# Rotary halves stacked, convolution taps in PSUM and on TensorE, and the memory's norm moved in a two-block transformer

## The reference

```python
def mla_mixer(x, ...):                    # 16 heads, 128 + 64 (rotary) columns
    ...
    scores = (jnp.einsum('bqhc,bkc->bhqk', ql, ckv)
              + jnp.einsum('bqhr,bkr->bhqk', qr, k_rope)) * scale
    probs = jax.nn.softmax(scores.astype(jnp.float32), axis=-1)
    return jnp.einsum('bhqk,bkc->bqhc', probs, ckv)

def diff_attention(q, k, v, lam):         # 4 heads, two components of 64 each
    ...
    sc = jnp.einsum("bhcqd,bhckd->bhcqk", q_blk, k) * scale
    sc = jnp.where(mask, sc, -jnp.inf)    # causal
    p = jax.nn.softmax(sc, axis=-1)
    a = p[:, :, 0] - lam * p[:, :, 1]
    return jnp.einsum("bhqk,bhkv->bhqv", a, v)

def hybrid_mixer(h, ...):
    ...
    q = partial_rope(q, positions)        # k likewise
    a = rmsnorm(diff_attention(q, k, v, lam), subln_g) * (1.0 - lam_init)
    c = u[..., :CV_WIDTH] * jax.nn.sigmoid(u[..., CV_WIDTH:])
    c = causal_dwconv(c, cv_dw_w) + cv_dw_b      # 512 channels, 31 taps
    c = jax.nn.silu(layernorm(c, cv_ln_g, cv_ln_b))
    return jnp.concatenate([a, c], axis=-1) @ w_out

def cross_attention(h, m, w_cq, w_ckv, w_co):    # m = rmsnorm(mem, norm_mem_g)
    kv = jnp.einsum("bmd,de->bme", m, w_ckv)
    ...
```

## Time and profile before

| | |
|---|---|
| median of three runs | 2626.41 us (2624.59 to 2631.72) |
| the profiled execution | 2628.91 us, its span 2627.1 us |
| granted clock of TensorE, mean over the span | 0.95 |
| busy, TensorE and VectorE | 2420.0 and 1550.6 us |
| busy, GpSimd and ScalarE | 1421.2 and 683.7 us |

### The profile page before, as it was taken

How to read it: one execution, slowest core, us unless ns; L and a number is a source line. 1 busy time by engine, 2 the same in 40 slices (tenths; PEclk the granted TensorE clock), 3 DMA queues, 4 the chain that set the end, 5 groups by cost and what they waited for, 6 DMA issues and landing times.

```text
span 2627.1 us, 26738 instructions
## 1 busy us (share of the span) xinstructions
PE 2420.0 (92%) x10646; PEld 1921.7 (73%) x10646; DVE 1550.6 (59%) x1870; ACT 683.7 (26%) x1223; POOL 1421.2 (54%) x845
## 2 busy tenths in 40 slices
PE   7999988999988899999899999886688899999997
PEld 5888866888876567777778888764466678778786
DVE  6785739335566455155755337678786645655555
ACT  3332322100023355255211001231123322211112
POOL 5445345666646213413466666555976564666663
PEclk9999999999999799899999999997777999999999
DMA  4222222333322101101233333231111232233332
GB/s 146 69 65 76 62 72 76 93 99 97 97 73 68 34 31 48 55 31 56 73 94 97 97 98 97 72 96 48 41 40 49 65 104 65 88 96 97 90 98 77
DMA packets 57436, 199.02 MB, mean 76 GB/s; under 512 B 6368, under 2 KB 7648, under 8 KB 57312
## 3 DMA queue, kind: packets, MB, share of 16 engines
q1 hardware_dynamic: 56160, 194.69, 24.3%
q10 hardware_dynamic: 1152, 2.62, 0.3%
HBM read 195.19 MB, written 2.10 MB: 75 GB/s over the span
## 4 chain that ended last, share of the span: by engine, by line
PE 79%; DVE 14%; ACT 3%; POOL 1%; issue 1%; DMA 0%; DVEq 0%; ACTq 0%; SPq 0%; POOLq 0%
PE bank L393 24%; PE bank L394 23%; PE bank L395 23%; DVE d_acc L1606 3%; DVE uL L1598 2%; PE bank L741 1%; PE bank L736 1%; POOL wL L2315 1%; PE bank L557 1%; PE bank L751 1%; DVE tmp L1598 1%; DVE sums L1598 1%; DVE mq L1598 1%; DVE tmp L1606 1%; PE bank L538 1%
## 5 line engine op out<-in xcount | busy, mean ns | idle before, releaser
L2313 POOL TENSOR_SCALAR wH<-raw 128x1024 fp32r<-128x1024 f32 (+3 forms) x375 | 403.3, 1075 | 1134.2 <-PE bank L395 1106.2
L2315 POOL TENSOR_TENSOR wL<-raw,wH 128x1024 fp32r<-128x1024 f32 (+3 forms) x375 | 910.8, 2429 | 31.3
L393 PE MATMUL bank<-aH,wH 128*128 128x512 f32 x1520 | 615.9, 405 | 73.7 <-ACT aH L1060 36.9
L394 PE MATMUL bank<-aL,wH 128*128 128x512 f32 x1520 | 602.5, 396 | 0.0
L395 PE MATMUL bank<-aH,wL 128*128 128x512 f32 x1520 | 602.3, 396 | 0.0
L393 PE MATMUL bank<-uH,wH 128*128 128x512 f32 x960 | 381.0, 397 | 32.1 <-DVE uL L1598 26.7
L393 PEld LDWEIGHTS bank<-aH,wH 128*128 128x128 f32 x1520 | 292.9, 193 | 150.1 <-issue 36.3
L394 PE MATMUL bank<-uL,wH 128*128 128x512 f32 x960 | 377.9, 394 | 0.0
L395 PE MATMUL bank<-uH,wL 128*128 128x512 f32 x960 | 377.7, 393 | 0.0
L394 PEld LDWEIGHTS bank<-aL,wH 128*128 128x128 f32 x1520 | 292.6, 193 | 65.0 <-issue 4.7
L395 PEld LDWEIGHTS bank<-aH,wL 128*128 128x128 f32 x1520 | 291.4, 192 | 63.1
(11 more groups left out here) (292 smaller groups left out, 3347.6 us busy)
## 6 DMA issues: line engine op xcount, KB each, us to landing
raw<-in_ws SPq DMA_DIRECT2D x341, 512.0 KB, 3.5
raw<-in_ws SPq DMA_DIRECT2D x16, 384.0 KB, 3.0
raw<-in_ws SPq DMA_DIRECT2D x9, 256.0 KB, 2.6
h<-in_xT SPq DMA_DIRECT2D x4, 512.0 KB, 7.0
out<-c_F SPq DMA_DIRECT2D x8, 256.0 KB, 2.1
raw<-in_ws SPq DMA_DIRECT2D x8, 192.0 KB, 2.6
tmp<-in_pT ACTq DMA_DIRECT2D x4, 256.0 KB, 2.8
d_P<-in_memT ACTq DMA_DIRECT2D x2, 512.0 KB, 4.6
```

The source lines that it names most:

```text
L393: P.e.matmul(o, lH, rH, start=start, stop=False, skip_group_check=skip)
L394: P.e.matmul(o, lH, rL, start=False, stop=False, skip_group_check=skip)
L2313: G.e.tensor_scalar(wH[n % NW][:, c], raw[n % NR][:, c], 1.0, 0.0, MUL, ADD).then_inc(*G.did("wH", n, i))
L2315: G.e.tensor_tensor(wL[n % NW][:, c], raw[n % NR][:, c], wH[n % NW][:, c].bitcast(F32), SUB).then_inc(*G.did("w", n, i))
```

## The change

**Latent attention.** Per head one tile m_qr[i] holds the high part of the rotary columns in one half of the partitions and the low part in the other; m_krH and m_krL hold the keys' columns in both halves. Two matmuls of 128 rows replace the three of 64. Per pair of heads ScalarE and VectorE do one half-height operation more. The division by the sum goes from ScalarE to GpSimd, four instructions per head, put into GpSimd's queue ahead of a chosen weight split.

The scaling ahead of the permutation is gone, and nearly every instruction has one operand in a bank. The core of the diff:

```diff
@@ scores, TensorE
-                    P.e.matmul(b.ap[:, :], m_qrH[r, c], m_krH[r, :], start=False, stop=False)
-                    P.e.matmul(b.ap[:, :], m_qrH[r, c], m_krL[r, :], start=False, stop=False)
-                    P.e.matmul(b.ap[:, :], m_qrL[r, c], m_krH[r, :], start=False, stop=True).then_inc(*P.did("ms", hd, n))
+                    P.e.matmul(b.ap[:, :], m_qr[hd % 2][:, c], m_krH[:, :], start=False, stop=False)
+                    P.e.matmul(b.ap[:, :], m_qr[hd % 2][:, c], m_krL[:, :], start=False, stop=True).then_inc(*P.did("ms", hd, n))
@@ GpSimd
+            def divide(hd):
+                for n in range(4):
+                    x = m_P[hd % 2][:, n, :]
+                    G.wait_ge(V, "minv", hd, n)
+                    G.e.tensor_scalar(x, x, m_st[:, 4 * (hd % 2) + n, 2:3], 0.0, MUL, ADD).then_inc(*G.did("mP", hd, n))
...
             for n in range(len(PLAN)):
+                if n in divided:
+                    divide(divided[n])
                 split_chunk(n, 2 if n == 0 else 1)
-                for _ in range(200 if n == last else after.get(n, 0)):
-                    next(tap, None)
@@ end of the second MLP's layer, TensorE
                 stat_end("ple", i)
                 P.also("end ple", i)
+                if i == 1:
+                    for o in range(4):
+                        memory_keys(o)
@@ taps, VectorE
+                for i in range(3):
+                    y = bk_acc(i)
                     for k in range(31):
+                            V.wait_ge(V, "tap", i, k - 1)
+                            stt(y, x, wk, y, MUL, ADD).then_inc(*V.did("tap", i, k))
@@ taps of tile 3, TensorE
+                for k in range(k0, k1):
+                    P.wait_ge(A, "dg", k)
+                    P.e.matmul(taps["bank"].ap[:, :], d_dg[k % 4][:, :], d_cp[:, BY_PE, 2 + k:514 + k], start=k == 0, stop=k == 30,
+                               skip_group_check=True).then_inc(*P.did("ctap", k))
@@ rotation, VectorE
+                stt(y, y, s, C[:, :], MUL, MUL).then_inc(*V.did("rc", j))
+                V.wait_ge(P, "rts", j)
+                stt(t, bk("rts", j)[:, :], s, Sn[:, :], MUL, MUL).then_inc(*V.did("rts", j))
+                V.wait_ge(V, "rts", j)
+                tt(y, y, t, ADD).then_inc(*V.did("rr", j))
@@ order of a head, TensorE
             for hd in range(3):
                 d_turned(hd)
                 d_scores(hd + 1)
                 if hd < 2:
-                    rotated(2 * hd + 4)
-                    rotated(2 * hd + 5)
+                    rotary_in(2 * hd + 4)
+                    rotary_in(2 * hd + 5)
+                    memory_keys(4 + hd)
+                    rotate(2 * hd + 4)
+                    rotate(2 * hd + 5)
+                conv_taps(8 + 8 * hd, min(16 + 8 * hd, 31))
                 d_values(hd)
```

More of the change, by code:

```diff
@@ L289, in build, with mlp_memory @@
         mlp_r, mlp_q, mlp_E, tab = [], [], [], []
-        for i in range(2):
+        def mlp_memory(i):
             with ExitStack() as st:
@@ L294, in build @@
                 mlp_E.append(sb(f"E_{i}", [128, 8, T], F32, st))
[L295 removed]
+                tab.append([sb(f"tab{j}_{i}", [128, T], F32, st) for j in range(3)] if i == 0 else
+                           [mlp_E[1][:, 5 + j, :] for j in range(3)])
+        mlp_memory(0)
         with ExitStack() as st:
@@ L1309, in rotate @@
                     A.wait_ge(P, "ms", hd - 1, 3)
-                do(m_qrH[:, :], tmp[1][:, :], ACT.Copy).then_inc(*A.did("qrH", hd))
+                for i in range(2):
+                    j = do(m_qr[i][half_rows(i), :], tmp[1][half_rows(i), :], ACT.Copy)
+                j.then_inc(*A.did("qrH", hd))
             def heads_in(hd):
@@ L1955, in rotate @@
                 V.wait_ge(A, "qrH", hd)
-                low(m_qrL[:, :], tmp[1][:, :], m_qrH[:, :]).then_inc(*V.did("qrL", hd))
+                for i in range(2):
+                    j = low(m_qr[i][half_rows(1 - i), :], tmp[1][half_rows(i), :], m_qr[i][half_rows(i), :])
+                j.then_inc(*V.did("qrL", hd))
             def heads_in(hd):
@@ L2058, in some_taps, with memory_keys @@
                     next(tap, None)
+            def memory_keys(o):
+                V.wait_ge(A, "xkH", o)
+                low(x_kL[:, o, :], bk("xk", o)[:, 0:256], x_kH[:, o, :]).then_inc(*V.did("xkL", o))
+            for o in range(4):
+                memory_keys(o)
             V.wait_ge(A, "rstd", "n", 1)
             for i in range(4):
-                t = tmp[(i + 1) % 2][:, :]
+                a, b = bk("ca", i)[:, :], bk("cb", i)[:, :]
                 V.wait_ge(P, "cb", i)
-                if i == 3:
-                    V.wait_ge(A, "memH", 6)
@@ L2206, in dve @@
             residual("z", "wo", ("z",), lambda k: vv("norm_cross_g_2", k))
-            for o in range(8):
-                V.wait_ge(A, "xkH", o)
-                low(x_kL[:, o, :], x_kF[:, o, :], x_kH[:, o, :]).then_inc(*V.did("xkL", o))
             for half in range(2):
```

505 lines of the change are left out of this document (256 added, 249 removed).

## The result

The changed kernel takes 2549.61 us (median of four runs, 2549.08 to 2551.4) where the kernel before took 2625.62 on the same chip (four runs, 2624.59 to 2631.72): a ratio of 0.9707, with a 95% interval of 0.969 to 0.9724. That is 76 us less, where 98 were forecast. The execution whose profile is read here took 2551.4 us, with a span of 2549.6, so 77.5 less than the profiled one of before.

What follows compares the result with a forecast made beforehand. TensorE was taken to bound latent attention, VectorE's taps differential attention and convolution. Terms -40 + 11 - 33 - 36 = -98 took 2628.9 to 2531, less 2.5 for the median: 2528 us; own range 2512 to 2545, wider 2492 to 2570.

Steps and rivals of the forecast that it cites:

- (a): Rival, latent attention scores: switches don't cost what was thought, so the scores save only 19 us; 2549 us, chance 0.10.
- (c): Rival, differential attention loop: five banks instead of eight give the taps' gain back, loop stays at 193; 2549 us, chance 0.15.
- (1): Latent attention scores: five 128-row matmuls per tile instead of six with switches between 128 and 64 rows; 40 us saved.
- (2): Latent attention: the division of the probabilities moves from ScalarE to GpSimd at no cost.
- (e): Rival, latent attention: GpSimd, waiting for a head's sums, delivers the next split 2 us late per head; 2560 us, chance 0.05.
- (4): Gate's sum to norm's sum: four key tiles put ahead take weight slots, so splits come later; +11 us.
- (5): Norm's sum to differential attention's first scores: VectorE's taps in banks at 0.80 us each; 33 us saved.
- (b): Rival, convolution taps: in a bank they are held by GpSimd as before, 1.3 us each; 2562 us, chance 0.13.
- (f): Rival, slower: VectorE instructions writing a bank are far dearer than ones only reading it; 2665 us, chance 0.03.
- (6): First differential attention scores to the projection's first three tiles: more TensorE work but less standing, 172 us; 36 saved.
- (3): Second MLP: the memory's norm moves there beside a full TensorE; costed at 0 to 1 us.
- (7): After the projection: the key split lies beside full TensorE work; 0 to 2 us, taken as 0.

Runs made afterwards that it cites:

- e1: The changed kernel with the latent attention's rotary stacking taken back (six score matmuls per tile, three of 64 rows); 2593.12 us.
- e2: The changed kernel with the division of the probabilities back on ScalarE; 2545.7 us.
- v2: The changed kernel with memory key tiles moved, differential attention's scores over 128 rows and the division back on ScalarE; 2519.19 us.
- v1: The changed kernel with memory key tiles moved and differential attention's scores over 128 rows; 2526.34 us.
- e5: The changed kernel with memory key tiles moved: one instead of four ahead of the mixer's norm, the others later; 2534.95 us.
- e3: The changed kernel with VectorE's convolution taps added up in SBUF instead of in two banks; 2566.21 us.
- e4: The changed kernel with differential attention's scores over 128 rows, each component's keys zero-padded in the other half; 2541.17 us.
- e6: The changed kernel with 30 of TensorE's 31 tap matmuls cut to a quarter of their columns; 2544.37 us.

## Why the prediction was right, and where its size was off

**Right in direction and in its places.** The gain is VectorE's waiting taken out of differential attention and convolution and TensorE's switches taken out of the scores, as said. The time itself, 2549.6, lies outside the forecast's own 2512 to 2545, on the figure of rivals (a) and (c), and within the wider range only because that reaches over them; neither rival's cause is borne out. By the terms:

(1) Scores, -40 forecast, -35.9 measured. The 1.13 us per tile show the mechanism, and e1 that it is the switch and not a part common to all matmuls. The Trainium skill, "TensorEngine Tiling (Array Packing)", section Key Properties, says that a change of mode drains TensorE; e1 agrees. Work at full clock fell by 37 us (315.7 to 278.5) and the loss to half clock by 11, but idle time rose by 12 (6.6 to 18.9): VectorE's low parts m_knL and m_krL came late. About half of that is the division's doing: with it back on ScalarE (e2) the idle time is 12.4 and the stretch 42.2 us shorter than before. The 11 us of clock and the idle time were not in the sum, so that the total came so near to 40 is in part luck.

(2) "Cost: nothing" was wrong by 4 to 7 us (e2, and v2 against v1). I had looked for the price on GpSimd and in the chain of a head, where the division fits (698 ns in the trace, 0.62 assumed). It lay on VectorE, whose operations with two SBUF inputs take up to 1.6 times as long beside it. Rival (e)'s place was wrong too: it is not the splits that come late.

(4) +11 forecast, +13.9 measured; the reason holds: splits come one by one, and TensorE waits for them 6.0 us in three pieces. They came 4.2 us apart (L400's first matmuls 1702.94 and 1707.13), not 3.8. VectorE's additions ran beside them, but that these are the cause wasn't tested. e5 takes 10 us of the term away, but not by the slots alone: 8.7 us of it is TensorE's busy time, the work of three key tiles put elsewhere, and the waits for splits (6.0 us) are replaced by the norm's own (5.2 us).

(5) -33 forecast, -39.1 measured. The tap took 755 ns instead of 0.80 beside GpSimd's splits (busy 42.4 of 71.7 us): rivals (b) and (f) are out. e3 shows the mechanism: the bank is worth 16.5 of the 39 us. What the rest owes to the memory's norm, put elsewhere, and to GpSimd's taps, left out, wasn't taken apart.

(6) -36 forecast, -15.7 measured: here is the error. The step was: "Laid out in the order of the instructions ... 165, and with some half clock 172". Its work was right (140 forecast, 140.8 measured), and so was its waiting (25 in the layout, 22.6 measured). The clock was not: the layout has 7 us for it, and it took 28.9. Before, 41.2 us were lost to half clock beside 47.8 us of waiting, and the layout let most of that loss go away with the waits. In part this is right: of the seven falls of the clock in the changed kernel five begin in or behind a wait. But the first two begin in the 64-row scores of heads 0 and 1 with TensorE busy throughout, and behind the waits, too, the clock stays low through the scores of heads 2 and 3. These scores the change leaves as they are. e4, which changes only them, brings 19 of the 29 us back.

Rival (c)'s number for the loop, 193, is what was measured (192.3), yet not by its cause. The waits that show the banks are the last transposes' (L892), 5.4 us in all, and the layout had 25 us of waiting where 22.6 came; the 20 us by which the loop is too long are clock. The last sign of being wrong, waits for banks that come free late, is there in this small measure. That the two engines "overlap no better than now" is not so either: idle time has halved.

(2), (3) and (7) added nothing in the sum; all the rest of the kernel changed by -0.7 us, so (3) and (7) hold as a sum; taken singly they weren't measured.

Open is what in the scores lowers the clock: the 64 rows or the changes between 64 and 128 rows, which e4 takes away together. That the matmuls are short is not enough, since those of e4 are as short; nor is it enough that 64-row matmuls and such changes occur, since in the latent attention of before, with both in every score tile, the clock is 1.00 over 60 us.

## What to carry to other kernels

Price a stretch at the clock that its own matmuls have shown, not at full clock plus a little: where the profile shows half clock while TensorE has no gap, taking waits away won't bring the clock back, but another shape of the same matmuls may. So look at each fall of the clock by itself, and at what TensorE did ahead of it. Before an operation moves to an engine with spare time, look at whose memory inputs it will run beside, not only at the queue it joins. And where weights pass through a few slots, work moved into a gap takes its slots along; count how late the next ones come.

## What was not expected of the hardware

- The clock fell to 0.50 only 4.2 us into head 0's 64-row scores, after 19.8 us without a gap at 1.00 (windows of the changed kernel); with the same products on 128 rows, half of them zeros, it stayed at 1.00 (e4, where TensorE was busy 5.08 of the 7.90 us). In the latent attention the 64-row form had 33.2 us busy at half clock where the stacked one has 8.1 (e1); there the falls begin behind waits, and differ in how long they last.
- With 19.6 us of TensorE's work taken out, its mean clock fell from 0.83 to 0.79 and only 5.2 us were gained: the two new falls begin where TensorE waits for the diagonal weights (e6).
- A VectorE instruction that reads and writes a bank costs hardly more than one that only reads it: 694 to 699 ns in the rotation, 752 as a tap, against 687.
- GpSimd's division by a column of factors, 698 ns for 128x512, raised VectorE's tmp<-tmp beside it from 692 to 1125 ns (e2).
